# Expert units 50 to 127 of a PEER layer: joined 512-column first products, a VectorE sum, and two elementwise jobs on GpSimd

## What is computed

```python
def peer_ffn(h, wq, sub_keys, u_table, v_table):
    q = (hf @ wq).reshape(t, PEER_HEADS, 2, PEER_HALF)
    ...
    top_v, top_i = lax.top_k(sc, PEER_TOPK)
    ...
    best_v, best_pos = lax.top_k(cand, PEER_TOPK)
    ...
    gate = jax.nn.softmax(best_v, axis=-1)
    ...
    def block(args):
        xb, eb, gb = args
        u = jnp.take(u_table, eb, axis=0)
        act = jax.nn.gelu(jnp.einsum('phkd,pd->phk', u, xb).astype(jnp.float32), approximate=False)
        ...
```

## Time and profile before

| | |
|---|---|
| median of 3 runs | 2352.18 us (2349.55 to 2353.56) |
| the profiled execution, its time | 2350.93 us |
| its span, first to last instruction | 2348.8 us |
| mean granted TensorE clock | 0.986 of full speed |
| busy: PE, PEld, DVE, ACT, POOL | 96%, 85%, 68%, 50%, 2% |

### The profile page before, as it was taken

One profiled execution on the slowest core, in us unless ns is written; L12 is line 12 of the kernel. 1 busy time (PEld: TensorE's weight loads), 2 busy tenths in 40 slices (PEclk: granted clock), 3 DMA queues, 4 the chain that ended last, 5 costly groups with the idle time before them and its releaser, 6 DMA issues. The chain is left out here.

```text
span 2348.8 us, 36404 instructions
## 1 busy us (share of the span) xinstructions
PE 2245.6 (96%) x14300; PEld 2005.0 (85%) x14300; DVE 1607.9 (68%) x2800; ACT 1177.1 (50%) x2052; POOL 57.1 (2%) x28
## 2 busy tenths in 40 slices
PE   8988999999999999999998999999999999979998
PEld 8877788999999998888877888988888788868887
DVE  7867546999889985666666556666657555776555
ACT  5522444455554445555555445445443544575444
POOL 0131000111000000000000000000000000000000
PEclk9989999999999999999999999999999999999999
DMA  6462324355444445555536546536555655404552
GB/s 266 144 72 96 137 97 163 117 188 179 147 150 146 145 148 178 195 192 193 196 127 242 197 179 235 198 126 217 188 193 181 245 185 191 148 1 162 197 184 102
DMA packets 78306, 390.18 MB, mean 166 GB/s; under 512 B 9771, under 2 KB 12715, under 8 KB 49740
## 3 DMA queue, kind: packets, MB, share of 16 engines
q1 hardware_dynamic: 76684, 383.59, 45.7%
q0 software_dynamic: 1040, 4.19, 1.6%
q10 hardware_dynamic: 432, 0.33, 0.0%
HBM read 382.83 MB, written 5.24 MB: 165 GB/s over the span
## 5 line engine op out<-in xcount | busy, mean ns | idle before, releaser
L251 DVE TENSOR_TENSOR split_slots<-ring,split_slots 128x1024 fp32r<-128x1024 f32 x404 | 482.2, 1239 | 137.2 <-ACT split_slots L242 137.0
L2873 PE MATMUL banks<-x_transposed,split_slots 128*128 128x512 f32 x1360 | 481.1, 397 | 2.0 <-PEq L454 2.0
L402 DVE SCALAR_TENSOR_TENSOR expert_lo<-ring,expert_hi 128x512 fp32r<-128x512 f32 x512 | 363.5, 715 | 173.8 <-ACT expert_hi L397 172.9
L242 ACT ACTIVATE split_slots<-ring 128x1024 fp32r<-128x1024 f32 x404 | 403.0, 1050 | 155.5 <-PE banks L393 139.4
L397 ACT ACTIVATE expert_hi<-ring 128x512 fp32r<-128x512 f32 x512 | 323.2, 632 | 267.2 <-PE banks L393 267.2
L2874 PE MATMUL banks<-x_transposed,split_slots 128*128 128x256 f32 x1360 | 382.0, 281 | 0.0
L2873 PEld LDWEIGHTS banks<-x_transposed,split_slots 128*128 128x128 f32 x1360 | 256.0, 188 | 63.7 <-issue 2.2
L391 PE MATMUL banks<-x_transposed,expert_hi 128*128 128x256 f32 x1024 | 296.9, 290 | 5.5 <-DVE expert_lo L402 5.5
L392 PE MATMUL banks<-x_transposed,expert_hi 128*128 128x256 f32 x1024 | 290.7, 284 | 0.0
L393 PE MATMUL banks<-x_transposed,expert_lo 128*128 128x256 f32 x1024 | 290.6, 284 | 0.0
L2874 PEld LDWEIGHTS banks<-x_transposed,split_slots 128*128 128x128 f32 x1360 | 257.6, 189 | 1.5
(11 more groups left out here) (484 smaller groups left out, 4154.6 us busy)
## 6 DMA issues: line engine op xcount, KB each, us to landing
ring<-in_ffn_w SPq DMA_DIRECT2D x132, 1024.0 KB, 4.8
ring<-in_peer_u SPq DMA_DIRECT2D x128, 512.0 KB, 3.3
ring<-in_peer_v SPq DMA_DIRECT2D x128, 512.0 KB, 3.4
ring<-in_w_in SPq DMA_DIRECT2D x16, 1024.0 KB, 5.4
ring<-in_sgu_w_in SPq DMA_DIRECT2D x16, 1024.0 KB, 4.9
ring<-in_peer_wq SPq DMA_DIRECT2D x8, 1024.0 KB, 5.7
ring<-in_sgu_w_out SPq DMA_DIRECT2D x8, 1024.0 KB, 4.8
ring<-in_kv_w SPq DMA_DIRECT2D x6, 1024.0 KB, 4.8
```

The source lines that it names most:

```text
L242: act.activation(self.parts[:, b, 0, p], self.k.w.slot(g)[:, p], ACT.Copy).then_inc(self.high_done, 1)
L251: ins = dve.tensor_tensor(self.parts[:, b, 1, p], self.k.w.slot(g)[:, p], self.parts[:, b, 0, p].bitcast(F32), ALU.subtract)
L402: return dve.scalar_tensor_tensor(dst, src, scale, hi.bitcast(F32), ALU.mult, ALU.subtract)
L2873: pe.matmul(out(j, slice(0, 2 * SEQ)), lh, k.xT.both[:, c, :, :], start=(c == 0), stop=False)
```

## The change

For units 50 to 127 four things are different.

1. The high part meets both parts of x in one matmul of 512 columns (`k.xT.both`, L2171 of the changed kernel), which fills a whole PSUM bank: columns 0 to 255 get high x high, 256 to 511 high x low. The low part's matmul of 256 columns (L2172) is added to the first half. A chunk has two matmuls instead of three.
2. The bank's two halves must then be added. VectorE does it with a reduction of 512 columns to 256 into the tile `gelu` (`add_halves`, L2414); the gelu on ACT reads this tile and no longer PSUM, so it waits for VectorE.
3. The gate multiplication goes from VectorE to GpSimd (L2326).
4. The low part of the second half of units 53 to 128 goes from VectorE to GpSimd (`pool_low`, L2069), behind the gate multiplication of the unit two before it.

The core of the diff:

```diff
+        self.by_pool = range(FIRST_SCATTER + 3, KEYS + 1)
...
-            sp.wait_ge(self.low_done, 2 * (n - 6) + 2)
+            for half in range(2):
+                self.split_ready(sp, n - 6, half)
...
+    def split_ready(self, engine, n, half):
+
+        if half == 1 and n in self.by_pool:
+            engine.wait_ge(self.pool_low_done, n - self.by_pool[0] + 1)
+        else:
+            ours = min(max(n - self.by_pool[0], 0), len(self.by_pool))
+            engine.wait_ge(self.low_done, 2 * n + half + 1 - ours)
+
+    def pool_low(self, pool, n):
+        pool.wait_ge(self.high_done, 2 * n + 2)
+        hi, lo = self.halves(n, 1)
+        pool.tensor_tensor(lo, self.landing(n, 1), hi.bitcast(F32), ALU.subtract).then_inc(self.pool_low_done, 1)
...
+            def u_joined(m):
+                if m - 2 >= FIRST_SCATTER:
+                    pe.wait_ge(summed, m - 1 - FIRST_SCATTER)
+                else:
+                    pe.wait_ge(gelus, m - 1)
+                for half in range(2):
+                    tiles.split_ready(pe, m, half)
+                    hi, lo = (part.rearrange("p (c n) -> p c n", c=DC // 2) for part in tiles.halves(m, half))
+                    for c in range(DC // 2):
+                        at = half * DC // 2 + c
+                        pe.matmul(k.psum[:, 6 + m % 2, :], hi[:, c, :], k.xT.both[:, at, :, :], start=(at == 0), stop=False)
+                        ins = pe.matmul(product(m), lo[:, c, :], k.xT.hi[:, at, :], start=False, stop=(at == DC - 1))
+                    ins.then_inc(tiles.eaten, 1)
...
             def activate(m):
-                act.wait_ge(tiles.eaten, 2 * m + 2)
+                if m < FIRST_SCATTER:
+                    act.wait_ge(tiles.eaten, 2 * m + 2)
+                    src = product(m)
+                else:
+                    act.wait_ge(summed, m + 1 - FIRST_SCATTER)
+                    src = gelu[:, m % 2, :]
...
+            for m in range(FIRST_SCATTER + 1, KEYS):
+                gate_block(m)
+                if m + 2 in tiles.by_pool:
+                    tiles.pool_low(pool, m + 2)
...
+            def add_halves(m):
+                dve.wait_ge(tiles.eaten, 2 * m + 2)
+                if m - 2 >= FIRST_SCATTER:
+                    dve.wait_ge(gelus, m - 1)
+                    if scattered_before(m - 2) > 0:
+                        dve.wait_ge(gated, m - 2 - FIRST_SCATTER)
+                dve.tensor_reduce(gelu[:, m % 2, :], k.psum[:, 6 + m % 2, :].rearrange("p (a n) -> p n a", a=2), AX_X, ALU.add
+                                  ).then_inc(summed, 1)
...
             for m in range(FIRST_SCATTER, KEYS):
-                fill(2 * (m + 3))
-                fill(2 * (m + 3))
+                fill(2 * m + 5)
+                add_halves(m)
                 for g in scattered_after(m + 2):
                     if g >= next_group:
                         onehots_of(g)
-                if scattered_before(m) > 0:
-                    gate_block(m)
+                if m + 2 in tiles.by_pool:
+                    lows[0] += 1
+                else:
+                    fill(2 * m + 6)
                 for g in scattered_after(m):
                     multiply(g, m + 1)
```

More of the change, by code:

```diff
@@ L2026, in __init__ @@
         self.lo = k.sb(ctx, "expert_lo", [P, 2, D], F32R)
-        self.high_done, self.low_done, self.eaten = (k.sig.new() for _ in range(3))
+        self.high_done, self.low_done, self.eaten, self.pool_low_done = (k.sig.new() for _ in range(4))
+        self.by_pool = range(FIRST_SCATTER + 3, KEYS + 1)
         self.first = 2 * ((g0 + PEER_HEADS) % RING)
@@ L2106, in pick_and_run_experts @@
         STEPS = 35
+        summed = k.sig.new()
         @block.sync
@@ L2148, in u_products @@
                 for half in range(2):
-                    pe.wait_ge(tiles.low_done, 2 * m + half + 1)
+                    tiles.split_ready(pe, m, half)
                     hi, lo = (part.rearrange("p (c n) -> p c n", c=DC // 2) for part in tiles.halves(m, half))
@@ L2183, in v_products @@
                 for half in range(2):
-                    pe.wait_ge(tiles.low_done, 2 * n + half + 1)
+                    tiles.split_ready(pe, n, half)
                     hi, lo = tiles.halves(n, half)
@@ L2199, in _ @@
             for m in range(KEYS):
-                u_products(m)
+                if m < FIRST_SCATTER:
+                    u_products(m)
+                else:
+                    u_joined(m)
                 if m == DEPTH + 1:
@@ L2219, in activate @@
             def activate(m):
-                act.wait_ge(tiles.eaten, 2 * m + 2)
+                if m < FIRST_SCATTER:
+                    act.wait_ge(tiles.eaten, 2 * m + 2)
[3 more added lines that the diff above has]
+                    src = gelu[:, m % 2, :]
                 seen = GROUP * scattered_before(m)
+                if seen < SEQ:
+                    ins = act.activation(acts[:, m, seen:], src[:, seen:], ACT.Gelu)
                 if seen > 0:
[L2223 to L2227, removed]
+                    ins = act.activation(gelu[:, m % 2, 0:seen], src[:, 0:seen], ACT.Gelu)
                 ins.then_inc(gelus, 1)
@@ L2283, in _, with gate_block @@
                                    ALU.mult).then_inc(chosen, 1)
+            def gate_block(m):
+                seen = GROUP * scattered_before(m)
+                pool.wait_ge(gelus, m + 1)
+                own = acts[:, m, 0:seen]
+                pool.tensor_tensor(own, gelu[:, m % 2, 0:seen], own, ALU.mult).then_inc(gated, 1)
+            for m in range(FIRST_SCATTER + 1, KEYS):
+                gate_block(m)
+                if m + 2 in tiles.by_pool:
+                    tiles.pool_low(pool, m + 2)
         @block.vector
```

## The result

The changed kernel took 2390.39 us as the median of four runs (2389.64 to 2392.14), the kernel before 2351.61 in the same comparison: a ratio of 1.0164, 95% interval 1.0147 to 1.0181. It is 39 us slower. The prediction was 2405 us within 2360 to 2438, slower with a chance of 0.90.

A forecast was written before the change was run, and what follows sets the result against it. TensorE bounds units 50 to 127 before the change, VectorE after: 223 us own list, 106 GpSimd holds and 6 at units without one-hots make 335 against 282; with small terms +54 on 2350.9 gives 2405 us, range 2360 to 2438.

The forecast's parts named there:

- TensorE's gain: Units 50 to 127: two matmuls a chunk at the SwiGLU pairs' 0.353 us instead of 0.36 save 4 us.
- VectorE's own list: VectorE's low parts, sums, one-hots and `multiply` in the 78 changed units: together 223 us of 282, so lighter.
- the slow-read bound: VectorE's sum, hopping between bank halves, could cost up to 0.95 us instead of 0.60: up to +27 us.
- The exclusion: GpSimd holds VectorE's low parts and one-hots for whole instructions, 2.16 ns a column: 106 us; `multiply` and sum escape.
- The hold of a low part: Each GpSimd low part of 512 columns holds VectorE 1.11 us; 76 of them make 84 us.
- The gate's hold: GpSimd's gate multiplications, 10,388 columns at 2.16 ns, hold VectorE 22 us, 0.29 us per unit.
- Where it falls: Both GpSimd jobs fall into VectorE's one-hots, none hidden under `multiply` or sum: 4.66 us per unit with a group.
- let in at the next instruction's end: GpSimd jobs arriving during VectorE's one-hots start when the running instruction ends, then hold VectorE for their whole length.
- My first rival: Row one-hots not excluded, so `multiply` hides beneath GpSimd's low part: 3.94 us a unit, 2368 us; chance 0.20.
- Units without a group: The 16 units without one-hots take 3.5 us, waiting for ScalarE's high part and GpSimd's low part: 6 us more.
- The one that ended at no loss: GpSimd falls into VectorE's gaps, TensorE still bounds: 2353 us, 2348 with the chain hidden too; chance 0.10.
- The clock: With TensorE waiting in every unit its clock could fall; at 1.2 GHz throughout, 2639 us; chance 0.03.

The follow-up runs named there:

- 3: The changed kernel with GpSimd filling the same tiles with zeros instead of multiplying and subtracting, all waits kept: 2343.12 us, ratio 0.9959.
- 8: The changed kernel with one-hots reading key numbers from PSUM and VectorE's sum before its low part: 2347.22 us, ratio 0.9987; repeated, 2349.49 us, ratio 0.9992.
- 4: The changed kernel with one-hots reading the key numbers from a copy in a free PSUM bank: 2353.67 us, ratio 1.0017.
- 2: The changed kernel with three 256-column products as before and no sum, gate and second-half low parts still on GpSimd: 2352.2 us, ratio 1.0012.
- 9: The changed kernel with GpSimd making the low part of unit m+2 before the gate multiplication of unit m: 2375.95 us, ratio 1.0110.
- experiment 1: The changed kernel with gate and all low parts back on VectorE, GpSimd idle, joined products and sum kept: 2376.03 us, ratio 1.0117.
- 7: The changed kernel with the column one-hot made before the four row one-hots: 2395.96 us, ratio 1.0193.
- 10: The changed kernel with VectorE's sum before its remaining low part, key numbers still in SBUF: 2382.67 us, ratio 1.0144.
- experiment 6: The changed kernel with the gate back on VectorE behind the one-hots, only second-half low parts on GpSimd: 2381.66 us, ratio 1.0132.

## Why the prediction was right, and what was off

*TensorE's gain.* Predicted 4 us from the pace of the SwiGLU pairs, 0.353 us. Where TensorE bounds (3 and 8), it takes 8.3 us less from the first gelu to the last. But some 2 of these are there only because the first gelu comes later: from unit 50's first matmul to the first of the second products it is 285.8 us before, 279.3 in 3 and 280.0 in 8, 6 us less. The pace was right. With writes only, six pairs come every 0.35 us:

```profile
764.61 0.28 PE L2172 MATMUL banks<-x_transposed,expert_lo 128*128 128x256 f32 x1
...
766.70 0.28 PE L2172 MATMUL banks<-x_transposed,expert_lo 128*128 128x256 f32 x1
```

Units without a group went from 2.88 us to 2.82 (units 124 to 126, by the gelus of 3), as this pace says. Units with a group went from 3.77 to between 3.67 and 3.71; the prediction had 3.69 and 3.63, 0.04 to 0.08 us too little. Right in sign, a third too small.

*VectorE's own list.* The sum's cost was right (0.68 us, 0.60 from start to start), and the hop through PSUM cost nothing; the slow-read bound was not needed.

*The exclusion.* Right, and it decides. It was read from two places of the profile before, 448 and 475 us; 4 shows it by a single operand, 2 shows it for row one-hots, which no row before did. So VectorE and GpSimd do not meet only at semaphores, as the section on the core has it. Here the trace now agrees with what the Trainium skill's "SBUF — State Buffer", section "Who interferes with whom", says of two SBUF inputs, of `tensor_scalar` and of reductions. The hold of a low part was 1.11 us predicted and is 1.81 - 0.68 = 1.13. The gate's hold was overestimated: 0.40 us at 244 columns (four row one-hots in 1.50 instead of 1.10 at 894 us), 0.2 at 160, nothing below 50, where 2.16 ns a column would give 0.53, 0.35 and 0.1.

*Where it falls.* This is the step that was off. "Nothing of GpSimd's work hides under the two instructions that could hide it" holds from 780 us on; a unit there, 4.76 us on average with `multiply`, has the predicted 4.66 us. Until 776 us, in units 51 to 94, the gate is so small that the column one-hot starts first, and `multiply` hides part of the low part: 3.9 to 4.1 us. These are 38 units with a group. They took 151.6 us, where the prediction's times (4.66 us, 4.23 where no `multiply` follows) make 174.5: 23 us that did not come. All other units together took some 3 us more than predicted. The forecast was only 15 us off because its sum was also too small by its own unit times: 52 x 4.66 + 10 x 4.23 + 16 x 3.5 = 341 us, not 335 (12 of the 16 units without one-hots have a `multiply` all the same, and ten with one-hots have none). That part is luck. This is the order that I had written down, down to the 0.2 us between 1.03 (start of the column one-hot) and 1.2 (the low part's request), and had then not followed: "let in at the next instruction's end" meant the end of the column one-hot, behind which `multiply` is free. My first rival, 3.94 us a unit, had that timing for another reason, and the measured time lies between the two cases. 9 shows that this place alone is worth 14 us: with the gate out of the way the late units go at the early units' pace.

*Units without a group.* Predicted 3.5 us, and the profile has 3.58 (two low parts on GpSimd at 749.95 and 753.53), rising to 3.75 late. In the reading of what costs what, though, I gave the sum's wait for ScalarE's high part too little: experiment 1 has 17 us of it, at 1.1 us a unit.

*The rivals.* The one that ended at no loss, GpSimd's work under the gaps, is what 8 makes true by moving an operand and one instruction; it came out at 2347 to 2349, where it had been put at 2348 with the chain of waits hidden too. The clock did not fall: 1.00 in the window at 820 us with TensorE busy for 34 of 40 us.

## What to carry to other kernels

Before an elementwise job goes from VectorE to GpSimd, count as VectorE's own time what GpSimd will take, for every VectorE instruction nearby that reads two SBUF operands or runs from SBUF to SBUF at the higher rate of the earlier trace rows (1024 columns in 0.752 us). Work moved so came back as large or larger: some 0.8 us a unit went off the list, and units with a group took 0.8 us more than VectorE's list in the first half and 1.3 to 1.5 in the second. Look for an operand that can live in PSUM: it took 37 of 39 us back. A saving on the engine that bounds has to be set against the slack of the next one, here 0.2 us a unit for a sum of 0.6, and the order of independent instructions around a shared resource is worth 6 to 14 us here (7, 9, 10), since 0.02 us decides who is first.

## What the runs showed of the hardware that I had not expected

- An exclusion turns a smooth change of sizes into a step: between the groups with a gate of 152 and of 160 columns the unit's time went from 4.12 to 4.64 us.
- A GpSimd instruction that only writes holds no VectorE instruction with two SBUF inputs (in experiment 3 fills lay beside nearly all column one-hots, and the longest of these was 0.691 us), but a row one-hot did wait for one: 0.760 us at most, against 0.343 in the median.
- A waiting GpSimd instruction is not always next. Between the column one-hot and a gate on VectorE, in experiment 6, the gate went first from 649 us on; in units without a `multiply` the next low part on VectorE went ahead as well, and GpSimd's record grew to 2.36 us and more (1.29 alone).
- A row one-hot that reads PSUM lasts 0.396 us instead of 0.336, and the column one-hot 0.675 instead of 0.682. For the column one-hot the memory of this operand changes hardly anything but the exclusion; the row one-hot also loses 0.06 us.
